# Zeros for the token buffers of a routed layer: stored during the dense layer instead of during the attention

## The reference, cut to what matters

```
hn = rms_norm(h, attn_norm[0]);  h = h + mla(hn, ...)
hn = rms_norm(h, ffn_norm[0]);   h = h + (silu(hn @ w_gate) * (hn @ w_up)) @ w_down
hn = rms_norm(h, attn_norm[1]);  h = h + multiscale_pool(hn, pool_w, pool_scale)
hn = rms_norm(h, ffn_norm[1]);   h = h + moe_swiglu(hn, router, w_gate, w_up, w_down)
return rms_norm(h, final_norm)
```

## Time and profile before

| | |
|---|---|
| three executions, median (lowest, highest) | 1180.32 us (1179.08 to 1180.77) |
| profiled execution, its own time | 1184.12 us |
| its span, first to last instruction | 1182.5 us |
| PE busy | 1103.1 us (93%) |
| DVE, ACT, POOL busy | 385.7, 278.1, 57.1 us |
| mean granted clock of TensorE | 0.981 of full speed |

### The profile page before, as it was taken

How to read it: one execution, slowest core, us unless ns; L and a number is a source line. 1 busy time by engine, 2 the same in 40 slices (tenths; PEclk the granted TensorE clock), 3 DMA queues, 4 the chain that set the end, 5 groups by cost and what they waited for, 6 DMA issues and landing times.

```text
span 1182.5 us, 19051 instructions
## 1 busy us (share of the span) xinstructions
PE 1103.1 (93%) x7414; PEld 1002.0 (85%) x7414; DVE 385.7 (33%) x703; ACT 278.1 (24%) x533; POOL 57.1 (5%) x99
## 2 busy tenths in 40 slices
PE   5999999799999999999997899999999999999980
PEld 4878877688888888888786799999999999999980
DVE  5586672354244442453564001010101010101015
ACT  5445552242224222232340001010101010101011
POOL 2210110000000000000002000000000000000002
PEclk9999999899999999999998999999999999999995
DMA  7027758434415144151203999999999999999996
GB/s 254 17 91 196 215 150 206 130 116 134 107 54 141 52 126 106 53 142 53 71 19 138 285 274 270 272 266 301 267 303 280 304 283 305 281 298 286 301 237 232
DMA packets 273230, 225.26 MB, mean 190 GB/s; under 512 B 29968, under 2 KB 246032, under 8 KB 273200
## 3 DMA queue, kind: packets, MB, share of 16 engines
q1 hardware_dynamic: 260192, 185.88, 56.2%
q0 software_dynamic: 11616, 36.32, 10.8%
q10 hardware_dynamic: 1392, 2.64, 0.6%
HBM read 198.43 MB, written 26.35 MB: 190 GB/s over the span
## 4 chain that ended last, share of the span: by engine, by line
PE 86%; DVE 6%; DMA 5%; ACT 1%; issue 1%; POOL 0%; DVEq 0%; SPq 0%; ACTq 0%; POOLq 0%
PE bank L1303 26%; PE bank L1317 14%; PE bank L905 13%; PE bank L907 13%; PE bank L906 13%; DMA scratch<-in_ffn_norm 2%; PE bank L1077 1%; PE bank L1364 1%; DMA stage_own<-in_moe_w_up 1%; PE bank L917 1%; PE bank L1281 1%; PE bank L1207 1%; PE bank L1057 1%; PE bank L1068 1%; PE bank L1292 1%
## 5 line engine op out<-in xcount | busy, mean ns | idle before, releaser
L1303 PE MATMUL bank<-scratch,stage_own 128*128 128x128 f32 (+1 forms) x2720 | 327.5, 278 | 8.4 <-DMA stage_own<-in_moe_w_gate 3.0
L1303 PEld LDWEIGHTS bank<-scratch,stage_own 128*128 128x128 f32 x2720 | 318.2, 191 | 10.5 <-DMA stage_own<-in_moe_w_gate 3.4
L1821 DVE TENSOR_TENSOR qr_now<-krT,bank 128x128 f32<-128x128 f32 (+1 forms) x80 | 23.4, 292 | 378.1 <-ACT krT L855 378.1
L1317 PE MATMUL bank<-qr_now,stage_own 128*128 128x128 f32 (+1 forms) x1152 | 143.5, 278 | 0.0
L1317 PEld LDWEIGHTS bank<-qr_now,stage_own 128*128 128x128 f32 x1152 | 137.3, 192 | 0.0
L905 PE MATMUL bank<-big_hi,w_lo 128*128 128x512 f32 (+2 forms) x352 | 134.4, 382 | 0.0
L907 PE MATMUL bank<-big_hi,w_hi 128*128 128x512 f32 (+2 forms) x352 | 134.3, 381 | 0.0
L906 PE MATMUL bank<-big_lo,w_hi 128*128 128x512 f32 (+2 forms) x352 | 134.2, 381 | 0.0
L855 ACT ACTIVATE krT<-bank 128x128 f32<-128x128 f32 (+1 forms) x80 | 22.5, 281 | 376.9 <-PE bank L1303 376.9
L1390 DVE TENSOR_TENSOR w_lo<-stage_own,w_hi 128x1024 fp32r<-128x1024 f32 (+1 forms) x91 | 105.4, 1203 | 14.0 <-ACT w_hi L608 13.9
L608 ACT CAST w_hi<-stage_own 128x1024 fp32r<-128x1024 f32 (+1 forms) x91 | 88.9, 1032 | 15.0 <-DMA stage_own<-in_mla_w_down 6.5
(11 more groups left out here) (243 smaller groups left out, 1146.5 us busy)
## 6 DMA issues: line engine op xcount, KB each, us to landing
stage_own<-in_moe_w_gate SPq DMA_DIRECT2D x82, 512.0 KB, 5.9
stage_own<-in_moe_w_up SPq DMA_DIRECT2D x82, 512.0 KB, 6.3
stage_own<-in_moe_w_down SPq DMA_DIRECT2D x72, 512.0 KB, 4.6
stage_own<-in_ffn_w_gate SPq DMA_DIRECT2D x21, 512.0 KB, 5.7
stage_own<-in_ffn_w_up SPq DMA_DIRECT2D x21, 512.0 KB, 6.9
stage_own<-in_ffn_w_down SPq DMA_DIRECT2D x21, 512.0 KB, 3.6
xbuf<-zeros POOLq DMA_DIRECT2D x2, 5184.0 KB, 41.9
scratch<-xbuf POOLq DMA_DIRECT2D x9, 576.0 KB, 6.3
```

Of the source, the lines that this page charges most:

```text
L1303: last = t_.matmul(dst[:, 0:n], w[:, k * P:(k + 1) * P], xT[:, k, 0:n], start=k == 0, stop=k == KD - 1)
L1317: last = t_.matmul(bank[4 + k // 3][:, col:col + n], w[0:parts, k * P:(k + 1) * P], e_act[0:parts, par, 0:n], start=first and k % 3 == 0, ...
L1821: v.tensor_tensor(e_act[:, par, 0:n], e_silu[:, par, 0:n], bank[2 * par + 1][:, 0:n], ALU.mult).then_inc(prod_ready, 1)
```

## The change

The three zero stores leave their place in POOL's stream and stand behind the loads of the mixer's gain and `pool_scale`. They wait for the last transpose of the dense layer's norm. Their source is no more the 128-column tile but 72 partitions by 1024 columns of `scratch` (the free `xn`), which POOL sets to zero just ahead (`zero_rows`). ACT gets a wait for all three stores ahead of the mixer's norm, which writes `xn` again.

```diff
+        zero_rows = scratch[0:ZP, 0:D]
...
+        zeros_ready = sem("zeros_ready")
...
-            pool.wait_ge(weight_lo, plan.unit("pair", 1, 1) + 1)
-            half = (JMAX + 2) // 2 * C
-            for rows in (xbuf[0:half, :], xbuf[half:, :], ybuf[E * C:, :]):
-                pool.dma_start(rows.rearrange("(p r) (c n) -> p (r c) n", p=ZP, n=P),
-                               zeros[0:ZP, :].unsqueeze(1).broadcast_to([ZP, rows.shape[0] // ZP * (D // P), P])
-                               ).then_inc(zero_stored, 16)
...
             pool.dma_start(pscale, a["pool_scale"].partition_broadcast(P).rearrange("p o d -> p (o d)")
                            ).then_inc(pscale_landed, 16)
+            pool.wait_ge(xnT_done, 2 * T)
+            g.memset(zero_rows, 0.0).then_inc(zeros_ready, 1)
+            pool.wait_ge(zeros_ready, 1)
+            half = (JMAX + 2) // 2 * C
+            for rows in (xbuf[0:half, :], xbuf[half:, :], ybuf[E * C:, :]):
+                pool.dma_start(rows.rearrange("(p r) n -> p r n", p=ZP),
+                               zero_rows.unsqueeze(1).broadcast_to([ZP, rows.shape[0] // ZP, D])).then_inc(zero_stored, 16)
             pool.wait_ge(xn_ready, 3 * T)
...
+            act.wait_ge(zero_stored, 48)
             for t in range(T):
                 act.wait_ge(h_ffn, 8 * (FI - 1) + 4 + t + 1)
                 norm_std(2 * T + t, t)
```

## The result

The changed kernel takes 1217.6 us (median of 4 runs, 1216.1 to 1221.0) against 1180.5 for the kernel before (median of 4 runs): a ratio of 1.032, 95% interval 1.0298 to 1.0344. The forecast was 1187.3 with a range of 1171 to 1200. So the sign is right and the size is not: 37 us were lost, not 7.

What follows compares the result with a forecast made beforehand. The prediction took PE, busy 1103.1 of 1182.5 us, to bound the kernel. Stalls and clock less the gain, 13.7 + 2.9 + 2 - 11.6 = +7.0 us, on the median 1180.3 gave 1187.3 us, range 1171 to 1200.

Steps and rivals of the forecast that it cites:

- The step to the dense layer: Step from attention to dense layer: PE waits of 2.7 and 6.0 us and 2.9 us of slow clock go, 11.6 us gained.
- Rival 3: Step to the dense layer: the wait stays as loads alone fill the engines; +18.6 us, 1199; chance 0.04.
- The attention: Where the zeros were stored before: PE busy 40.00 of 40.00 us, so nothing to be won there.
- POOL's part: POOL at the new place: memset 1.5 us at most, all three stores issued at once, nothing on the path.
- The place of the stall: Dense loop's next time: unit 1 lands late beside zeros, DVE's adds wait, PE's second half starts 13.7 us late.
- rival 1: Dense layer: the 17 us of slack holds, a pair takes under 0.14 us, whole gain stays; 1168.7 us; chance 0.17.
- the draw: Rival 2, dense layer: 0.18 to 0.22 us a pair, no second stall; 1178.9 or 1176.0 at 0.20; chance 0.21.
- The turn: Dense weight loads beside zeros: one weight packet and one zero packet take 0.25 us a pair, ends 0.20 and 0.29.
- The second stall: Unit 3 of the loop's next time lands late if zeros last: 2 us taken, ends 0 and 9.
- The clock: Behind the first stall in the dense layer PE runs at 1.2 GHz for some us: 2.9 us, 0 at the least.
- The zeros' own pace: Zero stores beside dense weights: 12 engines work, 0.25 us a row each, ending at about 306 to 326.

## Why the prediction was right in sign and wrong in size

- **The step to the dense layer: right.** 11.6 us forecast, 11.4 found; both waits gone, the clock at 1.00 there. The experiment with the gain on ACT's queue shows the cause for the larger of the two waits. Rival 3 (the wait stays) fell.
- **The attention: missed.** "Nothing is to be won there" was read from a busy share of 40.00 in 40.00. That stretch ended before the third store's issue at 169.37, behind which 2.7 of the 3.0 us were lost. The hold on DVE rests on coincidence in time, five times in three kernels, and on the kernel with 256 columns, where the zeros flow and no issue meets the scaling; no kernel took the hold away alone.
- **POOL's part: right.** The memset took 0.97 us (1.5 at the most), and the stores went out together, as forecast from the count of pieces.
- **The place of the stall: right.** ACT's long wait for units 0 and 1, then DVE's adds, then PE's second half, as in the chain of the earlier trace rows. "The slack holds" (rival 1) fell, and the draw with it.
- **The turn: wrong, and this is the step that failed.** "I take **0.25**", with 0.20 and 0.29 as ends, and from it "unit 1 lands at 262.05 + 2 + 128 x 0.25 = 296.1", 33 us behind its issue. It landed 68.6 us behind. Measured from unit 0's issue, with the prediction's 2 us of start, (317.3 - 247.7 - 2) / 128 = 0.53 us a turn. Put into the same working, 262.05 + 2 + 128 x 0.53 + 3 - 285.4 = 49.5 us, and the wait was 49.3: what hangs on unit 1 was seen rightly, and this factor was off. The rows that I drew it from had one store of zeros in flight, or the scatter, while further up I had written that all three would go out at once. "Three stores at once may bring it to 0.29" had no row behind it, and the cap of the range hung on it. The run with one store took (18.6 - 2) / 64 = 0.26 us a turn for unit 0: there the 0.25 was right.
- **Two things go into the 0.53.** The average pair was 0.37 and not 0.25. And a load is done when its slowest engine is, and the engines run far apart. The trace holds the time at which each of the 16 engines reports its part of a load. Of unit 0 the first came at 264.8, the eighth at 277.0 and the last at 297.9, 33 us apart; in the kernel before, with no zeros beside it, all sixteen come within 0.7 us. The slowest took (50.2 - 2) / 64 = 0.75 us a turn, twice the average. The queue row that stands behind this list says the same, for 248 to 298 us, while unit 0 was under way: 2163 packets are 135 an engine, and the slowest engine had just finished its 64. By bytes it is the same, 1.20 MB against the 0.52 of one unit. The uneven lie of the rows can be only a part of it: evenly laid, the sixteen parts of unit 0 still land 20 us apart with 48 partitions and 17 us apart with 96, where its slowest turn was (32.6 - 2) / 64 = 0.48 us and the average pair 0.24. Which engine is last, and why, the trace doesn't tell, and this stays open.
- **The second stall: 2 forecast, 0 found.** Zeros flowed until 332 us, but a first stall of this length let the next loads catch up. The clock: 2.9 forecast, 2.0 left over in the sum and 1.5 of it seen in PE's rows.

The weights' queue of the changed kernel from 248 to 298 us, in the columns of the earlier trace rows:

```profile
q1 hardware_dynamic: 2163, 1.20, 7.7%
```

So 11.6 - 13.7 - 2.9 - 2 stood where 14.4 - 49.3 - 2.0 came. The missing 30 us are the stall's size, 35.6, less the 3 in the attention and the 3 of the smaller terms. The zeros' own pace was overrated too. With 0.25 us a row on 12 engines I let them take until 306 to 326; with the dense layer 14.4 us sooner that is 292 to 312, and they took until 332.

## What to carry to other kernels

Before cutting a bulk transfer into fewer, larger descriptors, ask what its many small ones held back: here their number kept the stores single file, and with that gone three of them met the loads with the least slack. Price a load beside bulk traffic for as many transfers as will really be in flight, and by the engine that finishes last; where the trace has only one in flight, the range must be open upward. And place a bulk store behind the loads of a loop time: the same 15 MB that cost 37 us in front of them win 12 to 15 us against the kernel before in the gaps.

## What the runs showed of the hardware that was not expected

- A DVE scaling of 128x128 that takes 0.29 us took 2.34 and 3.50 us beside POOL's issues of a 10368-piece and a 9216-piece store, and 2.99 and 3.29 us in the kernel with the gain on ACT's queue. It ended some 0.05 us after the issue each time.

- SP's own issue stood for 34.41 us (the load issued at 254.72) while the engines were full. It looks as if a queue that can take no more holds the engine that issues, on SP as on POOL; no run tried that by itself.
- Even the load issued at 235.27, some 2 us behind the stores, took 17.0 us for its 512 KB; with one whole-row store beside it 11.6, and with small pieces flowing instead 3.7.
- The source's partitions bear on the pace of the zeros: 276 GB/s with 96 partitions against 194 with 48, each laid evenly over 16 engines, with three stores and the weights in flight. That the read side of the memory does this is argued, not shown.
- A load's sixteen parts, one an engine, land within 0.7 us of each other with no zeros beside it and 33 and 48 us apart beside three stores (units 0 and 1); the load counts as landed with the last.
